# A scan over two directions: twelve loads per batch are issued by GpSimd and not by the sync engine

## The chip, the cores and the metric

The kernel runs on one core of one Trainium2 chip. The metric is the device time of one execution in microseconds (us), and lower is better. The engines are TensorE (PE, matrix products; PEld is its weight load), VectorE (DVE), ScalarE (ACT), GpSimd (POOL) and the sync engine (SP), which here only issues transfers. All of them run their own instruction stream in order and wait for each other through semaphores. A transfer (DMA) is issued by an engine's stream and then moves its bytes beside it.

## The reference, cut to what matters

The program is a first block (an RWKV mixer with a short convolution, then a convolutional feed-forward part) and a second one (attention). The part around the change is the RWKV scan, which runs once forwards and once backwards over 256 context and 1024 sequence tokens, with 8 heads of 64:

```
def wkv_scan(state0, r, decay, kk, b, v, k, reverse):
    def step(S, inp):
        r_t, w_t, kk_t, b_t, v_t, k_t = inp
        sa = jnp.einsum("bhvk,bhk->bhv", S, kk_t)
        S = (S * w_t[:, :, None, :] - sa[..., None] * b_t[:, :, None, :]
             + v_t[..., None] * k_t[:, :, None, :])
        return S, jnp.einsum("bhvk,bhk->bhv", S, r_t)
    xs = tuple(jnp.swapaxes(t, 0, 1) for t in (r, decay, kk, b, v, k))
    S, ys = lax.scan(step, state0, xs, reverse=reverse)
    return S, jnp.swapaxes(ys, 0, 1)
```

Everything before it (projections of the normed input) and after it (output projection, feed-forward part, attention) is untouched.

## The kernel before, in words

The program is one function after another: `projections` (names with `b_`), `scan` (`c_`), `mix_up` (`e_`), then the rest. Between two of them all engines meet at a barrier.

`scan` does the recurrence in chunks of C = 64 tokens: STEPS = 20 steps, 4 of context and 16 of sequence, each for both directions x = 0 and 1. Within a chunk the recurrence needs the inverse of a 64x64 triangular matrix for every head and direction. The 20 steps are taken in NBATCH = 5 batches T of BATCH = 4 steps, and for each batch the 32x32 blocks of all its triangles are inverted together by VectorE, long before TensorE uses them:

- TensorE makes the triangles (`blocks`, L1235), ScalarE copies them to `c_raw`, SP stores them to `pb` (L1104) and loads them back one block per partition as `c_nb` (L1150).
- VectorE inverts in four parts (`blocks(T, part)`), one part behind the work of each of four steps. It writes `c_ui` and `c_ti`, the inverse and its transpose. The last part of batch T stands behind step 4T - 4.
- SP stores them to `ub` (L1154) and `tb` (L1156). In SP's `step(s)` this is done when (s + 3) % 4 is 0, so for s = 1, 5, 9, 13 and T = 1, 2, 3, 4.
- Twelve loads then scatter the blocks into the places where TensorE reads them: `load_inverse(T)`, that is 2 of `of_level` (L1098, into `c_td`) and 4 of `of_diag` (L1093, into `c_ud`) from `ub`, and the same from `tb`. Each of the twelve moves 64 KB as 32 partitions x 16 blocks x 32 numbers, so 512 runs of 128 bytes. Before the first six SP waits for the landing of `ub`, before the last six for that of `tb`. They increment a semaphore `inv{T % 2}_{x}`.
- TensorE's step s makes the products of step s and then those of the next step u = s + 1. `level_y(x, u)` (L1264, `c_ps<-c_td,c_lm`) is the first that reads `c_td` and `c_ud` of batch u // 4. It waits for all six loads of its direction x, so for u = 4, 8, 12 and 16, in steps 3, 7, 11 and 15, it needs what `load_inverse` of T = 1 to 4 brought.

The twelve loads of T = 0 are another matter: they are issued ahead of the steps, half by SP and half by ScalarE.

SP also loads the operands of step s + 2 in step s (`load`, L1120 `c_op` of 512 KB and L1121 `c_vz` of 128 KB, for each direction), and `load_inverse` stands in its stream ahead of the loads of the next step. `load` waits until TensorE has used the slot (`p_s`, `p_y`). After step 10 SP loads `c_hc`, after steps 11 and 17 `c_w_raw`, which GpSimd splits into a high and a low part (L1591 to L1598). SP's last loads of `c_w_raw` wait for these splits. Beside them and five clears at the start, GpSimd has nothing to do in `scan`.

Descriptors for transfers that GpSimd issues are kept in memory that the kernel reserves where it makes the program (the line is in both versions):

```
nc = bacc.Bacc("TRN2", target_bir_lowering=False, num_devices=1, dynamic_dma_scratch_size=1024)
```

Of the kernel before, what the change touches and what calls it, by code (L numbers as in the profile page):

```python
# [1032 lines left out]
def scan(nc, d, t):  # L1033

    DIRS, HEADS = range(2), range(2)
    ROWS = [slice(HEAD * h, HEAD * h + HEAD) for h in HEADS]
    BATCH = 4
    NBATCH = STEPS // BATCH
# [4 lines left out]
    with ExitStack() as st:  # L1043
        sem = Sems(nc, st, "c_")
# [28 lines left out]
        S = lambda name, x: sem(f"{name}{x}")  # L1073
# [16 lines left out]
        def of_diag(eng, T, x, src):  # L1090
            for h in HEADS:
                for b in range(2):
                    eng.dma_start(ud[x][T % 2][quarter(h, b), :, :, cols32(b)].rearrange("p j q c -> p (j q) c"),  # L1093
                                  d[src][T, x, h, b].rearrange("n r c -> r n c")).then_inc(S(f"inv{T % 2}_", x), 16)

        def of_level(eng, T, x, src):
            for h in HEADS:
                eng.dma_start(td[x][T % 2][level(x), :, :, cols32(h)].rearrange("p j q c -> p (j q) c"),  # L1098
                              d[src][T, x, h, x].rearrange("n r c -> r n c")).then_inc(S(f"inv{T % 2}_", x), 16)

        def store_raw_of(eng, T, x):
            for h in HEADS:
# [6 lines left out]
        @block.sync  # L1109
        def _(sp):  # L1110
            def wait(name, x, value):
                if value > 0:
                    sp.wait_ge(S(name, x), value)

            def load(x, u):

                slot = slot_of(x, u)
                wait("p_s", x, u - 2)
                wait("p_y", x, u - 2 - NCTX)
                sp.dma_start(op_ring[x][u % 3][:], d["ops"][x, :, slot]).then_inc(S(f"loaded{u % 3}_", x), 16)  # L1120
                sp.dma_start(vz[x][u % 3][OF_K[x]], d["vts"][slot].rearrange("(h p) q v -> p h (q v)", h=2)).then_inc(S(f"loaded{u % 3}_", x), 16)  # L1121

            def load_w1(n):
                if n >= 2:
                    sp.wait_ge(sem("w1_lo"), n - 1)
                done = sem(f"w1_raw{n}") if n < 3 else t["ahead"](f"w1_{n}")
                sp.dma_start(w1_raw[:, n % 2], d["w_out"][n // 2][:, n % 2, 0:KD // 2]).then_inc(done, 16)

            def load_conv():
                for k in range(KD // 2):  # L1130
                    sp.dma_start(hc[:, k, 1].bitcast(F32), d["mixd"][:, k]).then_inc(sem(f"hc{k}"), 16)

            def load_pre(i):
                for x in DIRS:
                    wait("p_pre", x, i - 3)
                    slot = min(slot_of(x, 2 * i), slot_of(x, 2 * i + 1))
                    sp.dma_start(pre_ring[x][i % 2][:].rearrange("p j q z -> p (j q) z"),
                                 d["ops"][x, :, slot:slot + 2, :, C:3 * C].rearrange("p j q z -> p (j q) z")).then_inc(S(f"pre{i % 2}_", x), 16)

            def store_raw(T):  # L1140

                for x in DIRS:
                    wait("raw", x, 2 * T)
                    store_raw_of(sp, T, x)

            def load_blocks(T):
                if T:
                    sp.wait_ge(sem("pb"), 128 * T)
                    sp.wait_ge(sem("w_last"), T)
                sp.dma_start(nb[:, 0:HB * HB], d["pb"][T].rearrange("x h b n r c -> (x h b n) (r c)")).then_inc(sem("nb"), 16)  # L1150

            def store_blocks(T):
                sp.wait_ge(sem("ui"), T + 1)
                sp.dma_start(d["ub"][T].rearrange("x h b n r c -> (x h b n) (r c)"), ui[:, 0:HB * HB]).then_inc(sem("ub"), 16)  # L1154
                sp.wait_ge(sem("ti"), T + 1)
                sp.dma_start(d["tb"][T].rearrange("x h b n r c -> (x h b n) (r c)"), ti[:, 0:HB * HB]).then_inc(sem("tb"), 16)  # L1156

            def load_inverse(T):

                for x in DIRS:  # L1160
                    wait("p_z", x, BATCH * (T - 1))
                sp.wait_ge(sem("ub"), 16 * (T + 1))
                of_level(sp, T, 1, "ub")
                of_diag(sp, T, 0, "ub")
                sp.wait_ge(sem("tb"), 16 * (T + 1))
                of_level(sp, T, 0, "tb")
                of_diag(sp, T, 1, "tb")

            def step(s):
                for x in DIRS:  # L1170
                    if s + 2 < STEPS:
                        load(x, s + 2)
                if s == 0:
                    store_raw(2)
                if s == 1:
                    load_blocks(2)
                if s - 1 in pres and pres[s - 1] % 2:
                    load_blocks(pres[s - 1] // 2)
                if (s + 3) % BATCH == 0 and s + 3 < STEPS:
                    store_blocks((s + 3) // BATCH)  # L1180
                    load_inverse((s + 3) // BATCH)
                if s == 10:
                    load_conv()
                if s == 11:
                    for x in DIRS:
                        wait("p_pre", x, 2 * NBATCH - 2)
                    for n in range(2):
                        load_w1(n)
                if s == 17:
                    for n in range(2, 5):  # L1190
                        load_w1(n)
                if s in pres:
                    if pres[s] % 2:
                        store_raw(pres[s] // 2)
                    if pres[s] + 2 < 2 * NBATCH:
                        load_pre(pres[s] + 2)

            load_blocks(0)
            for x in DIRS:
                load(x, 0)  # L1200
            load_pre(2)
            load_pre(3)
            for x in DIRS:
                load(x, 1)
            for h in HEADS:
                sp.dma_start(t["pend"][ROWS[h], 1, NCTX:SLOTS], d["pends"][ROWS[1 - h]]).then_inc(sem("pend"), 16)
            load_pre(4)
            load_pre(5)
            sp.wait_ge(sem("clear"), 4)
            store_blocks(0)  # L1210
            load_blocks(1)
            sp.wait_ge(sem("ub"), 16)
            of_level(sp, 0, 1, "ub")
            of_diag(sp, 0, 0, "ub")
            load_pre(6)
            load_pre(7)
            for s in range(STEPS):
                step(s)

        @block.tensor  # L1220
        def _(pe):
            def wait(name, x, value):
                if value > 0:
                    pe.wait_ge(S(name, x), value)
# [32 lines left out]
            def level_y(x, u):  # L1257

                wait("lm", x, 2 * u + 2)
                wait(f"inv{u // BATCH % 2}_", x, 96 * (u // BATCH // 2 + 1))  # L1260
                j = place(x, u)
                for q in range(PAIRS):
                    for h in HEADS:
                        mm = nc.tensor.matmul(first(bank[x][0])[quarter(h, 1 - x), q],  # L1264
                                              lm[x][u % 2][level(x), h, q, W_KK[x], cols32(1 - x)],
                                              td[x][u // BATCH % 2][level(x), j, q, cols32(h)], start=True, stop=True)
                mm.then_inc(S("p_yd", x), 1)
# [78 lines left out]
            for s in range(STEPS):  # L1346
                u, more = s + 1, s + 1 < STEPS
# [235 lines left out]
        @block.gpsimd  # L1583
        def _(pool):
            for x in DIRS:
                for par in range(2):
                    nc.gpsimd.memset(ud[x][par][:], 0.0).then_inc(sem("clear"), 1)
                nc.gpsimd.memset(sc[x][0][:], 0.0).then_inc(S("sc", x), 1)
            for k in range(KD // 2):
                pool.wait_ge(sem(f"hc{k}"), 16)  # L1590
                nc.gpsimd.tensor_copy(hc[:, k, 0], hc[:, k, 1].bitcast(F32)).then_inc(sem("hc_hi"), 1)  # L1591
                pool.wait_ge(sem("hc_hi"), k + 1)
                nc.gpsimd.tensor_tensor(hc[:, k, 1], hc[:, k, 1].bitcast(F32), hc[:, k, 0].bitcast(F32), ALU.subtract).then_inc(sem("hc_lo"), 1)
            for n in range(3):
                pool.wait_ge(sem(f"w1_raw{n}"), 16)
                nc.gpsimd.tensor_copy(w1_hi[:, n], w1_raw[:, n % 2]).then_inc(sem("w1_hi"), 1)
                pool.wait_ge(sem("w1_hi"), n + 1)
                nc.gpsimd.tensor_tensor(w1_lo[:, n], w1_raw[:, n % 2], w1_hi[:, n].bitcast(F32), ALU.subtract).then_inc(sem("w1_lo"), 1)  # L1598
# [2102 lines left out]
```

## Time and profile before

| what | value |
|---|---|
| median of 3 runs | 2266.69 us (2255.43, 2266.69, 2269.16) |
| the profiled execution, span from first to last instruction | 2265.7 us |
| mean granted TensorE clock in it | 0.957 of full |
| PE, DVE, ACT, POOL busy in it | 2050.2, 1500.4, 892.1, 773.6 us |
| transfers in it | 271.16 MB, mean 120 GB/s |
| `scan` in it (TensorE's first product of its steps to the barrier) | some 498 to 750 us |

The profile has no device time of its own for the profiled execution beside its span of 2265.7 us; the span is 1.0 us under the median of the runs. In the rows below a time is counted from the start of the span, the second number of a timeline row is its length, and an arrow in brackets names what ended the idle time before a piece.

### The profile page before, as it was taken

The numbers are of one execution on the slowest core, as the hardware profiler recorded it, in microseconds if no ns is written. First come the engines' busy times: TensorE is split into PE (matmuls) and PEld (weight loads), VectorE is DVE, ScalarE is ACT, GpSimd is POOL, SyncE is SP. The second block draws the span as 40 slices with busy tenths as digits, with TensorE's granted clock in tenths as the row PEclk, the third lists the DMA queues.
The fourth block names the chain that finished last, engine by engine and source line by source line (L and its number), as shares of the span: only waits on it lengthen the run. The fifth ranks groups of instructions, "written<-read, shape, count | busy, mean of one in ns | idle before, by whom it ended". The sixth has DMA issues, their size and how long they took to land. (4 is left out here: it accounts for less than half of the span.)

```text
span 2265.7 us, 37012 instructions
## 1 busy us (share of the span) xinstructions
PE 2050.2 (90%) x15072; PEld 1594.0 (70%) x15072; DVE 1500.4 (66%) x2052; ACT 892.1 (39%) x1445; POOL 773.6 (34%) x460
## 2 busy tenths in 40 slices
PE   4989999837878898999999979999899999999898
PEld 1767677636767676788877768887677776776566
DVE  5777767679774548788988870454746676546644
ACT  5453443414434637333333331443434354333320
POOL 1144433300030145877777724533321111111111
PEclk7999999958899999999999999999999999999899
DMA  7535444597655422122221274523211111102512
GB/s 308 182 122 174 151 141 130 154 264 197 167 177 143 159 75 75 56 84 84 84 76 73 84 272 139 177 73 122 85 56 56 66 38 47 66 19 84 195 47 84
DMA packets 181335, 271.16 MB, mean 120 GB/s; under 512 B 74280, under 2 KB 122024, under 8 KB 176816
## 3 DMA queue, kind: packets, MB, share of 16 engines
q1 hardware_dynamic: 164816, 250.57, 33.9%
q10 hardware_dynamic: 16352, 18.22, 2.7%
q8 instruction: 121, 1.98, 0.4%
q14 instruction: 46, 0.38, 0.1%
HBM read 200.53 MB, written 68.23 MB: 119 GB/s over the span
## 5 line engine op out<-in xcount | busy, mean ns | idle before, releaser
L105 PE MATMUL b_ps<-h_hi,b_wpool 128*128 128x512 f32 (+1 forms) x896 | 277.4, 387 | 10.8 <-POOL b_wpool L744 10.8
L2995 PE MATMUL g_ps<-g_h_hi,w 128*128 128x512 f32 x784 | 260.0, 403 | 6.0 <-ACT g_q L3192 5.9
L3313 POOL TENSOR_TENSOR w<-raw_down,w 128x1024 fp32r<-128x1024 f32 x38 | 94.5, 2488 | 464.6 <-ACT w L3168 464.6
L2262 DVE SCALAR_TENSOR_TENSOR e_vars<-grid,vec,e_vars 128x1024 f32<-128x1024 f32 x168 | 216.0, 1285 | 7.4 <-ACT e_vars L2009 4.2
L105 PEld LDWEIGHTS b_ps<-h_hi,b_wpool 128*128 128x128 f32 x896 | 167.8, 192 | 56.3 <-POOL b_wpool L744 14.4
L2995 PEld LDWEIGHTS g_ps<-g_h_hi,w 128*128 128x128 f32 x784 | 149.3, 190 | 40.8 <-ACT g_q L3192 6.9
L105 PE MATMUL b_ps<-h_lo,b_wpool 128*128 128x512 f32 (+1 forms) x448 | 170.6, 381 | 0.0
L2995 PE MATMUL g_ps<-g_h_lo,w 128*128 128x512 f32 x392 | 156.1, 398 | 0.0
L2674 POOL TENSOR_TENSOR g_down_lo<-raw_down,g_down_hi 128x1408 fp32r<-128x1408 f32 x26 | 86.7, 3339 | 142.5 <-ACT g_down_hi L2574 142.5
L2513 PE MATMUL g_pb<-g_z_hi,g_down_hi 128*128 128x512 f32 x286 | 114.8, 401 | 14.7 <-DVE g_down_lo L2751 9.8
L744 POOL TENSOR_TENSOR b_wpool<-raw_in,b_wpool 128x1024 fp32r<-128x1024 f32 x26 | 67.9, 2611 | 173.2 <-ACT b_wpool L530 173.2
L2513 PE MATMUL g_pb<-g_z_hi,g_down_lo 128*128 128x512 f32 x286 | 113.1, 396 | 0.0
L2513 PE MATMUL g_pb<-g_z_lo,g_down_hi 128*128 128x512 f32 x286 | 112.7, 394 | 0.0
L1989 ACT ACTIVATE e_main_hi<-e_raw_up 128x512 fp32r<-128x512 f32 x68 | 41.9, 622 | 171.2 <-DMA e_raw_up<-w_ffn 168.9
L2103 POOL TENSOR_TENSOR e_main_lo<-e_raw_up,e_main_hi 128x512 fp32r<-128x512 f32 x68 | 92.6, 1365 | 16.0 <-ACT e_main_hi L1989 16.0
L105 PEld LDWEIGHTS b_ps<-h_lo,b_wpool 128*128 128x128 f32 x448 | 86.0, 192 | 15.7 <-issue 1.0
L3090 PE MATMUL g_ps<-g_h_hi,w 128*128 128x512 f32 x224 | 78.5, 421 | 9.1 <-DVE g_sq L3473 3.3
L2995 PEld LDWEIGHTS g_ps<-g_h_lo,w 128*128 128x128 f32 x392 | 74.5, 190 | 16.2 <-issue 0.5
L3465 DVE COPY g_pt<-g_pb 128x512 f32<-128x512 f32 (+2 forms) x144 | 74.2, 552 | 16.6 <-PE g_pb L3056 15.5
L1473 DVE TENSOR_TENSOR c_lm<-c_ps,con_mixer 128x512 f32<-128x512 f32 x80 | 50.7, 684 | 48.6 <-PE c_ps L1253 48.3
L2311 DVE TENSOR_TENSOR e_z<-e_act_g,combine 128x512 f32<-128x512 f32 x42 | 63.9, 1561 | 21.3 <-ACT e_act_g L2022 21.3
L3222 ACT ACTIVATE g_s<-g_logits,g_mx 128x128 f32<-128x128 f32 (+7 forms) x64 | 49.7, 777 | 69.0 <-DVE g_mx L3446 67.5
(524 smaller groups left out, 5284.4 us busy)
## 6 DMA issues: line engine op xcount, KB each, us to landing
e_raw_up<-w_ffn SPq DMA_DIRECT2D x22, 1024.0 KB, 4.9
raw_down<-w_down SPq DMA_DIRECT2D x32, 704.0 KB, 4.2
c_op<-ops SPq DMA_DIRECT2D x40, 512.0 KB, 5.0
raw_down<-w SPq DMA_DIRECT2D x38, 512.0 KB, 3.7
raw_in<-w SPq DMA_DIRECT2D x26, 512.0 KB, 4.2
mod_stage<-ada_rows ACTq DMA_DIRECT2D x24, 512.0 KB, 3.7
zs<-e_z SPq DMA_DIRECT2D x21, 512.0 KB, 2.6
ops<-b_xin SPq DMA_DIRECT2D x20, 512.0 KB, 4.7
```

Source lines behind the costliest of these rows:

```text
L105: last = nc.tensor.matmul(out, w[:, k, :], x[:, k, cols], start=(k == 0 and n == 0), stop=(k == nk - 1 and n == 2))
L744: TT(weights(s)[1], raw, weights(s)[0].bitcast(F32), ALU.subtract).then_inc(sem("lo"), 1)
L1473: TT(lm[x][u % 2][:, h], quad(bank[x][h]), bc(t["c_tri"][:, x], 1, PAIRS), ALU.mult).then_inc(S("lm", x), 1)
L2103: TT(w_lo[slot], a_of[slot] if i < PLAIN else source[slot], w_hi[slot].bitcast(F32), ALU.subtract).then_inc(sem(f"w_lo{slot}"), 1)
L2262: STT(out=acc, in0=view, scalar=wt, in1=acc, op0=ALU.mult, op1=ALU.add).then_inc(sem("conv"), 1)
L2311: a = TT(z[:, cols(g)], act_g[:, cols(g)], val_of(g, i), ALU.mult)
L2513: mm = nc.tensor.matmul(bank_of(g, j), w[s][:, k], y[:, f], start=(f == 0 and i == 0), stop=(f == NFF - 1 and i == 2))
L2674: nc.gpsimd.tensor_tensor(w_lo[w_slot(n)], raw[:, n % 2], w_hi[w_slot(n)].bitcast(F32), ALU.subtract).then_inc(sem(f"w_lo{n % 2}"), 1)
L2995: mm = nc.tensor.matmul(out_bank, ww[w % 2][:, k], xx[g][:, k], start=(k == 0 and a == 0), stop=(k == KD - 1 and a == 2))
L3090: mm = nc.tensor.matmul(ps[1][:], ww[w % 2][:, k], xx[g][:, k], start=(a == 0 and b == 0), stop=(a == 1 + LAST and b == 2))
L3313: nc.gpsimd.tensor_tensor(w_lo[w % 2], raw[:, w % 2], w_hi[w % 2].bitcast(F32), ALU.subtract).then_inc(sem("lo"), 1)
L3465: nc.vector.tensor_copy(pt[:, h, at // P:to // P].rearrange("p b c -> p (b c)"), turned[u % 2][:, 0:to - at]).then_inc(sem("unturned"), 1)
```

## The change

`load_inverse` is taken out of SP's stream. GpSimd's stream now has the loads of T = 1, 2, 3 and 4 one batch after another, behind its clears and ahead of the splits of `c_hc` and `c_w_raw`. The waits inside it are the same. Each batch has semaphores of its own (`inv{T}_{x}`, counted to 96) where two were used in turn. SP's `step` keeps the two stores.

```
@@ of_diag, of_level
-                                  d[src][T, x, h, b].rearrange("n r c -> r n c")).then_inc(S(f"inv{T % 2}_", x), 16)
+                                  d[src][T, x, h, b].rearrange("n r c -> r n c")).then_inc(S(f"inv{T}_", x), 16)
...
@@ block.sync
-            def load_inverse(T):
-
-                for x in DIRS:
-                    wait("p_z", x, BATCH * (T - 1))
-                sp.wait_ge(sem("ub"), 16 * (T + 1))
-                of_level(sp, T, 1, "ub")
-                of_diag(sp, T, 0, "ub")
-                sp.wait_ge(sem("tb"), 16 * (T + 1))
-                of_level(sp, T, 0, "tb")
-                of_diag(sp, T, 1, "tb")
...
                 if (s + 3) % BATCH == 0 and s + 3 < STEPS:
                     store_blocks((s + 3) // BATCH)
-                    load_inverse((s + 3) // BATCH)
...
@@ block.tensor, level_y
-                wait(f"inv{u // BATCH % 2}_", x, 96 * (u // BATCH // 2 + 1))
+                wait(f"inv{u // BATCH}_", x, 96)
...
@@ block.gpsimd
                 nc.gpsimd.memset(sc[x][0][:], 0.0).then_inc(S("sc", x), 1)
+            def load_inverse(T):
+
+                for x in DIRS:
+                    if T > 1:
+                        pool.wait_ge(S("p_z", x), BATCH * (T - 1))
+                pool.wait_ge(sem("ub"), 16 * (T + 1))
+                of_level(nc.gpsimd, T, 1, "ub")
+                of_diag(nc.gpsimd, T, 0, "ub")
+                pool.wait_ge(sem("tb"), 16 * (T + 1))
+                of_level(nc.gpsimd, T, 0, "tb")
+                of_diag(nc.gpsimd, T, 1, "tb")
+
+            for T in range(1, NBATCH):
+                load_inverse(T)
             for k in range(KD // 2):
                 pool.wait_ge(sem(f"hc{k}"), 16)
```

On SP, around step 1, the stream before (the stores of T = 1, the twelve loads, then the operands of step 4):

```order
L1154 DMA ub<-c_ui 128x1024
L1156 DMA tb<-c_ti 128x1024
L1098 DMA c_td<-ub 32x16x32 x2
L1093 DMA c_ud<-ub 32x16x32 x4
L1098 DMA c_td<-tb 32x16x32 x2
L1093 DMA c_ud<-tb 32x16x32 x4
L1120 DMA c_op<-ops 128x1024
L1121 DMA c_vz<-vts 64x2x256
L1120 DMA c_op<-ops 128x1024
L1121 DMA c_vz<-vts 64x2x256
```

The same place on SP in the changed kernel:

```order
L1154 DMA ub<-c_ui 128x1024
L1156 DMA tb<-c_ti 128x1024
L1120 DMA c_op<-ops 128x1024
L1121 DMA c_vz<-vts 64x2x256
L1120 DMA c_op<-ops 128x1024
L1121 DMA c_vz<-vts 64x2x256
```

The operand loads of the next step now follow the stores at once; this is so at all four places.

On GpSimd, from its last clear on, before:

```order
L1588 MEMSET c_sc 128x256
L1591 CAST c_hc<-c_hc 128x1024
L1593 TENSOR_TENSOR c_hc<-c_hc 128x1024
L1591 CAST c_hc<-c_hc 128x1024
L1593 TENSOR_TENSOR c_hc<-c_hc 128x1024
```

And in the changed kernel, from the loads of T = 4 on (the same four rows stand three times ahead of them, for T = 1, 2 and 3):

```order
L1098 DMA c_td<-ub 32x16x32 x2
L1093 DMA c_ud<-ub 32x16x32 x4
L1098 DMA c_td<-tb 32x16x32 x2
L1093 DMA c_ud<-tb 32x16x32 x4
L1593 CAST c_hc<-c_hc 128x1024
L1595 TENSOR_TENSOR c_hc<-c_hc 128x1024
L1593 CAST c_hc<-c_hc 128x1024
L1595 TENSOR_TENSOR c_hc<-c_hc 128x1024
```

All 48 loads stand ahead of GpSimd's first split, which could start when `c_hc` had landed and now comes after batch 4.

## Rows read from the trace of the kernel before

**Rows 1.** The page: busy time and share of each engine, and the transfer queues.

```profile
PE 2050.2 (90%) x15072; PEld 1594.0 (70%) x15072; DVE 1500.4 (66%) x2052; ACT 892.1 (39%) x1445; POOL 773.6 (34%) x460
...
q1 hardware_dynamic: 164816, 250.57, 33.9%
q10 hardware_dynamic: 16352, 18.22, 2.7%
```

**Rows 2.** Windows: stretch, its us, busy us by engine, granted clock, DMA share, GB/s.

```profile
490.00:750.00 260.00, 203.41 (x5924) 178.24 (x5916) 185.52 (x343) 103.47 (x304) 22.03 (x14) 0.89 0.62 172
...
497.00:549.00 52.00, 38.80 (x1022) 34.03 (x1026) 49.44 (x97) 20.19 (x59) 0.00 (x0) 0.77 0.82 222
```

**Rows 3.** Waits in 490 to 745 us: total, times, longest.

```profile
PE c_ps L1264 <- DVE c_lm L1473: 11.3, 6, 6.7
PE c_ps L1264 <- DMA c_ud<-ub: 7.3, 1, 7.3
PE c_ps L1246 <- DMA c_vz<-vts: 2.4, 2, 1.4
PE c_ps L1264 <- DMA c_ud<-tb: 1.4, 1, 1.4
```

**Rows 4.** Timeline of SP: each batch's first loads, and batch 1's last group.

```profile
527.00 0.92 SPq L1098 DMA_DIRECT2D c_td<-ub  x2
...
531.14 3.29 SPq L1093 DMA_DIRECT2D c_ud<-tb  x4
...
573.80 0.85 SPq L1098 DMA_DIRECT2D c_td<-ub  x2
...
626.84 1.14 SPq L1098 DMA_DIRECT2D c_td<-ub  x2
...
682.46 2.04 SPq L1098 DMA_DIRECT2D c_td<-ub  x2
```

**Rows 5.** Timeline of TensorE: the first product that needs each batch.

```profile
549.62 0.28 PE L1264 MATMUL c_ps<-c_td,c_lm 32*32 32x32 f32 x5
...
604.60 0.61 PE L1264 MATMUL c_ps<-c_td,c_lm 32*32 32x32 f32 x32
...
655.04 0.81 PE L1264 MATMUL c_ps<-c_td,c_lm 32*32 32x32 f32 x32
...
704.55 0.82 PE L1264 MATMUL c_ps<-c_td,c_lm 32*32 32x32 f32 x32
```

**Rows 6.** DMA issues: issuing queue, count, KB each, median us from issue to landing.

```profile
c_ud<-ub SPq DMA_DIRECT2D x20, 64.0 KB, 2.4
...
c_ud<-tb ACTq DMA_DIRECT2D x4, 64.0 KB, 3.6
```

**Rows 7.** Line L1093: duration of an issue, and its time to landing (smallest, median, largest).

```profile
L1093 SPq DMA_DIRECT2D c_ud<-ub x20: 484/488/1236, 492.4 to 686.1; - x20
...
DMA to landing us min/median/max: 2.2/2.4/4.7
```

**Rows 8.** Timeline of TensorE after an idle time, and the same products later.

```profile
526.03 0.64 PE L1264 MATMUL c_ps<-c_td,c_lm 32*32 32x32 f32 x16 [6.73 <-DVE c_lm L1473]
...
529.87 1.97 PE L1246 MATMUL c_ps<-con,c_op 128*128 128x128 f32 x8
...
552.40 1.09 PE L1246 MATMUL c_ps<-con,c_op 128*128 128x128 f32 x8
```

**Rows 9.** Windows, columns as in Rows 2: the stretch after that idle time, and the next.

```profile
526.00:534.50 8.50, 7.91 (x152) 6.97 (x152) 7.99 (x31) 3.48 (x10) 0.00 (x0) 0.52 0.71 162
534.50:549.00 14.50, 12.28 (x408) 10.76 (x410) 13.57 (x24) 6.94 (x20) 0.00 (x0) 1.00 0.95 266
```

**Rows 10.** Timeline of GpSimd: its first split, its sixth and its last.

```profile
644.07 1.94 POOL L1591 CAST c_hc<-c_hc 128x1024 fp32r<-128x1024 f32 x1 [180.16 <-DMA c_hc<-mixd]
...
663.42 1.27 POOL L1598 TENSOR_TENSOR c_w_lo<-c_w_raw,c_w_hi 128x512 fp32r<-128x512 f32 x1
...
727.99 0.61 POOL L1596 CAST c_w_hi<-c_w_raw 128x512 fp32r<-128x512 f32 x1 [63.29 <-DMA c_w_raw<-w_out]
```

More of the change, by code:

```diff
@@ L1098, in of_level @@
                 eng.dma_start(td[x][T % 2][level(x), :, :, cols32(h)].rearrange("p j q c -> p (j q) c"),
-                              d[src][T, x, h, x].rearrange("n r c -> r n c")).then_inc(S(f"inv{T % 2}_", x), 16)
+                              d[src][T, x, h, x].rearrange("n r c -> r n c")).then_inc(S(f"inv{T}_", x), 16)
         def store_raw_of(eng, T, x):
```

## The prediction

> **What bounds the kernel now.** Read the engines first: TensorE is busy for 90% of the span, and all transfers come from two hardware queues, SP's and ACT's; GpSimd's has none [rows 1]. So nothing in this profile shows what a transfer issued by GpSimd costs, and that is the number on which everything below hangs. Then the stretch of the scan: in 260 us TensorE is busy for 203.41 and VectorE for 185.52, GpSimd for 22.03 [rows 2]. Neither engine is full, since each step is a chain that goes back and forth between TensorE, ScalarE and VectorE. A delay put into TensorE's stream there moves the end of the scan, and the barrier behind it hands this on to the rest of the kernel one for one.
>
> The waits say which delays come from transfers: TensorE waited 7.3 and 1.4 us for the scattered inverse, each once, both for batch 0, which the change leaves alone; and 2.4 us in two waits for the operands c_vz [rows 3]. For batches 1 to 4 it never waited. The reader is to see how much room there was: SP issued the first load of a batch at 527.00, 573.80, 626.84 and 682.46 us [rows 4], and the first product that needs the batch ran at 549.62, 604.60, 655.04 and 704.55 us [rows 5]. The differences are 22.6, 30.8, 28.2 and 22.1 us, 103.7 in all. These starts are not SP's to choose: they are when the store of ub had landed, so GpSimd cannot begin earlier, and its clears at the start of the scan are long over.
>
> **What is removed.** SP loses 12 issues in each of four batches. In batch 1 they fill 527.00 to 534.43 us [rows 4], 7.4 us. What stands behind them is the operand load of the next step. The most that can come of it is the two waits of TensorE for c_vz, 2.4 us [rows 3]. Where SP was late for no one, nothing is gained. The two stores of a batch stay on SP. The semaphores of their own cost nothing: the waits of TensorE are as many as before.
>
> **What is added.** GpSimd issues 48 loads, and waits for ub, tb and, for T above 1, for TensorE's p_z of the batch before the last, which is long done when ub lands. Let p be the time from one load to the next on GpSimd. TensorE's second direction needs the last of the twelve, so it stalls in a batch by 12p less the room of that batch. Below 22.1/12 = 1.84 us no batch stalls; above 30.8/12 = 2.57 us all four do, and the stall is 48p - 103.7 us. The sum is steep: a tenth of a microsecond in p is 4.8 us in the kernel.
>
> The bounds for p from rows: from below the issue on SP, 0.49 us [rows 7], if GpSimd only has to issue and the loads overlap as they do on SP. From above the longest landing of such a load, 4.7 us [rows 7], if each has to land before the next is made. I take the second picture, since the memory for descriptors that this kernel reserves is small, 1024 bytes, and each load is 512 runs. With one load at a time p is about a landing plus what comes ahead of it. The same load landed 2.4 us after its issue from SP and 3.6 us from ACT [rows 6]; I take the middle, 3.0 us. It is a choice: 2.4 is from a queue whose issue is cheap, and the 3.6 is from four loads at the start of the scan.
>
> The Trainium skill has the reason in "DMA: Bandwidth & Descriptors", sections "SWDGE vs HWDGE vs iDMA" and "Terms": a transfer issued by GpSimd has its descriptors written by software into a ring in SBUF, one queue of it, a descriptor being 16 bytes. By it 1024 bytes are an estimated 64 places for each of the 16 transfer engines and direction, and a load of 512 runs takes 32 of them and one for its completion, 33, so that two loads (66) do not fit. No row here shows this, as no row has such a queue.
>
> With p = 3.0 the twelve take 36 us, and the stalls are 13.4, 5.2, 7.8 and 13.9 us, 40.3 in all (48 x 3.0 - 103.7). One correction to it: the start of batch 2 at 573.80 us came late behind its store in a crowded moment, and with the stall of batch 1 ahead of it the crowd is another one. I take 2 us off.
>
> **What a stall costs beside itself.** After 6.73 us of idleness TensorE's eight transposes took 1.97 us against 1.09 later [rows 8]. The granted clock was 0.52 in the 8.5 us after it, which is the level of 1.2 GHz, and 1.00, 2.4 GHz, after that [rows 9]. TensorE was busy for 7.91 of these 8.5 us; at the full level this work takes 4.1, and as a part of it is hidden behind VectorE and ScalarE I count 3 us for a stall, 12 for four.
>
> **What the moved splits cost.** GpSimd's splits ran from 644.07 to 664.7 us and needed then 20.6 us [rows 10]. Now they wait for batch 4. With p = 3.0 that ends at 682.46 + 36 = 718.5 us on the old clock, the splits at 739, the last one, which needs one more load, at some 746; TensorE's scan ends 14 us later than before on the same clock, at 763. So they are hidden, with 17 us to spare, and a larger p moves both ends alike. The cover would be gone if the splits took twice their time beside VectorE. They no longer run beside VectorE at steps 11 and 12 but later: nothing either way.
>
> **The sum.** 40.3 - 2 + 12 = 50 us. The 2.4 us that SP could give back are not subtracted: both waits stand just ahead of a stall, which takes up what they free. The profiled span becomes 2265.7 + 50 = 2316 us. As this span is 1.0 us under the median of the runs, the forecast on the median is 2317 us, 2.2% slower.
>
> **The rivals.**
>
> *The loads overlap, and nothing happens.* If GpSimd makes the next load while the one before flies, p is its issue alone. Below 1.84 us there is no stall, and the time is 2266.7 - 2.4 = 2264 us at best, 2267 if the waits for c_vz turn into others. For it speaks that SP does just this (twelve in 7.4 us, each landing in 2.4), against it only the small descriptor memory. The Trainium skill speaks for this side, and for no effect: "DMA: Bandwidth & Descriptors", section "Issuing engines are not separate DMA queues", says that issuing from several engines saves only the sequencer's time, which is usually small. This is the case that ends on the other side of the forecast; the point from which it decides is p = 1.84 us.
>
> *One at a time, but quick.* At p = 2.4 (SP's median landing) the stalls are 6.2, 0, 0.6 and 6.7 us, and with the clock of two real stalls (6 us) the time is 2267 + 13.5 + 6 = 2286 us, just under 1%.
>
> *One at a time, and slow.* VectorE was busy for 49.44 of the 52 us in which batch 1 falls, and the transfer engines for 0.82 of them [rows 2]. If VectorE or the crowd holds up GpSimd, p = 4.0 gives 48 x 4.0 - 103.7 + 12 = 100 us, 2367 us; the bound 4.7 gives 134 us, 2401 us. In the Trainium skill, "SBUF — State Buffer", the box on the "DVE blocks DMA" trap says that VectorE's two-port instructions keep GpSimd from writing descriptors. VectorE's instructions here are mostly of another kind, and no row shows GpSimd held up by them.
>
> *A gain above 1%.* It would need 23 us, ten times what TensorE waited for any transfer that the change touches.
>
> **How the numbers follow.** One at a time with p from 2.6 to 3.6 us: 0.50 (48p - 103.7 + 10, so 31 to 79 us on 2267). Overlapping loads, no stall: 0.27. One at a time with p under 2.6: 0.11, half of it below 1%. Slow, p above 3.6: 0.11. A gain over 1%: 0.01. The range is from 2258 us (the no-stall case with the spread that the three runs show) to 2350 us, p = 3.6; it leaves out the slow case. A measurement of this kernel can tell about 1% from no change. Slower by over 1% is 0.50 + 0.11 + 0.06 = 0.67, within 1% 0.32, faster 0.01. The likeliest case alone has 2298 to 2346 us.
>
> **What would show it.** In the profile of the changed kernel GpSimd's loads should stand some 3 us apart, with 36 us from the first to the last landing of a batch, against 7.4 us of issue on SP. TensorE should wait at L1264 for a transfer into c_ud of tb in steps 3, 7, 11 and 15, longest in the first and the last, and its clock should drop behind each. The waits for c_vz should be gone, and SP should wait for GpSimd's split in step 17 for longer than before. The forecast is wrong if the loads stand less than 1.84 us apart, and its size is wrong by 48 times the error in p.

## The result and the profile after

The changed kernel takes 2328.62 us, the median of 4 runs (2326.62 to 2330.29), against 2267.93 us for the kernel before (4 runs, 2255.43 to 2273.80). The ratio is 1.0267, with a 95% interval of 1.0243 to 1.0292: 60.7 us slower. The profiled execution has a span of 2324.8 us, 59.1 more than the 2265.7 of before. The lines that TensorE, ScalarE and VectorE have in the scan stand 12 lower in the changed file: L1264, the product with c_td, is now L1252, L1246 is L1234, L1473 is L1461. GpSimd's splits stand two higher (L1591 is L1593).

The page of the changed kernel, busy time of the engines and the queues (they answer to [rows 1]). A queue written by software is new, with the 3.15 MB of the 48 loads; the work of TensorE, VectorE and ScalarE is what it was. GpSimd is busy for 27.3 us more: the 48 issues take 31.6 us, and its other work took 4.3 us less.

```profile
PE 2052.3 (88%) x15072; PEld 1598.8 (69%) x15072; DVE 1497.9 (64%) x2052; ACT 892.2 (38%) x1445; POOL 800.9 (34%) x508
...
q1 hardware_dynamic: 139472, 247.43, 32.1%
q10 hardware_dynamic: 16352, 18.22, 2.6%
q0 software_dynamic: 1536, 3.15, 0.5%
```

GpSimd's timeline in the changed kernel: parts of batch 1, the last loads of batch 4, and the first split behind them. Columns: start, duration, then in brackets the idle time before it and what ended that.

```profile
524.69 0.83 POOL L1098 DMA_DIRECT2D c_td<-ub  x1 [65.00 <-DMA ub<-c_ui]
531.34 0.66 POOL L1098 DMA_DIRECT2D c_td<-ub  x1 [5.82 <-issue]
533.94 0.65 POOL L1093 DMA_DIRECT2D c_ud<-ub  x1 [1.94 <-issue]
...
569.45 0.66 POOL L1093 DMA_DIRECT2D c_ud<-tb  x1 [1.84 <-issue]
...
759.07 0.65 POOL L1093 DMA_DIRECT2D c_ud<-tb  x1 [1.97 <-issue]
759.72 1.05 POOL L1593 CAST c_hc<-c_hc 128x1024 fp32r<-128x1024 f32 x1
```

The reader is to see "x1" in every row and the idle time between the rows. An issue keeps GpSimd for 0.65 us, and then it sits for 1.8 to 6.3 us before the next, though it waits for no semaphore there; that is why the view can say no more than "issue". From its first issue to its last a batch now takes 44.8, 36.5, 41.0 and 35.6 us, where SP issued batch 1 in 7.4. The split, which is no transfer, follows the last load without a gap: what holds GpSimd up stands in the way of its next transfer and not of its next computation.

TensorE's timeline, the products at which each direction needs the new batch, for batches 1 to 4 (answers to [rows 5]), and the first transposes behind the first stall:

```profile
556.08 0.63 PE L1252 MATMUL c_ps<-c_td,c_lm 32*32 32x32 f32 x16 [7.40 <-DMA c_td<-tb]
...
571.79 0.50 PE L1252 MATMUL c_ps<-c_td,c_lm 32*32 32x32 f32 x11 [15.08 <-DMA c_ud<-tb]
...
574.43 1.86 PE L1234 MATMUL c_ps<-con,c_op 128*128 128x128 f32 x8
...
622.71 0.44 PE L1252 MATMUL c_ps<-c_td,c_lm 32*32 32x32 f32 x16 [0.81 <-DMA c_td<-tb]
633.78 0.64 PE L1252 MATMUL c_ps<-c_td,c_lm 32*32 32x32 f32 x16 [10.63 <-DMA c_ud<-tb]
...
689.19 0.64 PE L1252 MATMUL c_ps<-c_td,c_lm 32*32 32x32 f32 x16 [3.87 <-DMA c_td<-tb]
699.52 0.64 PE L1252 MATMUL c_ps<-c_td,c_lm 32*32 32x32 f32 x16 [9.70 <-DMA c_ud<-tb]
...
751.22 0.64 PE L1252 MATMUL c_ps<-c_td,c_lm 32*32 32x32 f32 x16 [6.87 <-DMA c_td<-tb]
...
761.45 0.64 PE L1252 MATMUL c_ps<-c_td,c_lm 32*32 32x32 f32 x16 [9.59 <-DMA c_ud<-tb]
```

Each batch stops TensorE twice, first for the direction whose tb part is c_td, then for the other. Together these are 22.5, 11.4, 13.6 and 16.5 us, 64.0 in all, against none before. The waits of the scan (494.9 to 809 us; total, times, longest):

```profile
DVE c_lm L1461 <- PE c_ps L1241: 92.3, 30, 23.0
...
PE c_ps L1252 <- DMA c_ud<-tb: 47.4, 5, 15.1
...
PE c_ps L1252 <- DMA c_td<-tb: 19.0, 4, 7.4
...
PE c_ps L1252 <- DVE c_lm L1461: 5.5, 2, 4.9
```

One of the five waits for c_ud of tb, 2.4 us, is batch 0's. TensorE's waits for c_vz are gone, and its wait for VectorE's c_lm is 5.5 us where it was 11.3 [rows 3]. VectorE's own longest wait is now 23.0 us, where TensorE stands still for batch 1.

Now the scan cut at the stalls. First the kernel before, with the five stretches that end where each batch's first product ran (columns as in [rows 2]), its first stretch and the sum:

```profile
498.45:549.62 51.17, 39.42 (x1056) 34.56 (x1056) 48.68 (x92) 19.80 (x58) 0.00 (x0) 0.78 0.80 219
...
sum 252.53, PE 202.29 PEld 177.28 DVE 181.23 ACT 102.39 POOL 22.03; mean PE 40.46 PEld 35.46 DVE 36.25 ACT 20.48 POOL 4.41
```

The changed kernel, the same stretches without the stalls:

```profile
495.20:548.68 53.48, 42.00 (x1056) 36.94 (x1056) 50.49 (x96) 19.86 (x58) 4.11 (x6) 0.76 0.71 204
571.79:621.90 50.11, 43.72 (x1232) 38.99 (x1232) 33.31 (x70) 21.60 (x63) 5.23 (x8) 0.86 0.37 113
...
sum 247.34, PE 208.57 PEld 184.85 DVE 156.34 ACT 99.21 POOL 35.48; mean PE 41.71 PEld 36.97 DVE 31.27 ACT 19.84 POOL 7.10
```

And the four stalls alone:

```profile
548.68:571.79 23.11, 0.63 (x16) 0.56 (x17) 6.25 (x4) 1.36 (x3) 3.92 (x6) 0.57 0.66 168
...
sum 66.29, PE 2.36 PEld 2.07 DVE 23.78 ACT 3.28 POOL 15.37; mean PE 0.59 PEld 0.52 DVE 5.95 ACT 0.82 POOL 3.84
```

The sum closes: 66.3 us of stalls (the 64.0 us of waits and the few products between them), and 5.2 us less between them (252.5 to 247.3), so 61.1 us for the scan. The span grew by 59.1; the rest is that this execution reached the scan 3.25 us earlier and took 1.2 us longer behind it, small beside the spread of the runs of the kernel before (2255.43 to 2273.80).

### The profile page after: what moved, and what is told of

Read it like the earlier page. It is cut to its first block and busy times, and to the rows that moved or that the text cites. A ratio compares the mean times of both kernels' runs of the same rounds, so it can differ in the third digit from the quotient of the medians.

```text
span 2324.8 us, 37012 instructions
## 1 busy us (share of the span) xinstructions
PE 2052.3 (88%) x15072; PEld 1598.8 (69%) x15072; DVE 1497.9 (64%) x2052; ACT 892.2 (38%) x1445; POOL 800.9 (34%) x508
## 3 DMA queue, kind: packets, MB, share of 16 engines
q0 software_dynamic: 1536, 3.15, 0.5%
## 5 line engine op out<-in xcount | busy, mean ns | idle before, releaser
L105 PEld LDWEIGHTS b_ps<-h_hi,b_wpool 128*128 128x128 f32 x896 | 166.4, 190 | 55.7 <-POOL b_wpool L744 14.6
L2997 PEld LDWEIGHTS g_ps<-g_h_hi,w 128*128 128x128 f32 x784 | 149.1, 190 | 40.3 <-ACT g_q L3194 6.6
L2515 PE MATMUL g_pb<-g_z_hi,g_down_hi 128*128 128x512 f32 x286 | 115.1, 402 | 14.8 <-DVE g_down_lo L2753 9.8
L1461 DVE TENSOR_TENSOR c_lm<-c_ps,con_mixer 128x512 f32<-128x512 f32 x80 | 51.1, 685 | 92.4 <-PE c_ps L1241 92.3
L1252 PE MATMUL c_ps<-c_td,c_lm 32*32 32x32 f32 x640 | 18.1, 208 | 83.1 <-DMA c_ud<-tb 47.4
```

Of the source, the lines that this page charges most:

```text
L105: last = nc.tensor.matmul(out, w[:, k, :], x[:, k, cols], start=(k == 0 and n == 0), stop=(k == nk - 1 and n == 2))
L1461: TT(lm[x][u % 2][:, h], quad(bank[x][h]), bc(t["c_tri"][:, x], 1, PAIRS), ALU.mult).then_inc(S("lm", x), 1)
L2515: mm = nc.tensor.matmul(bank_of(g, j), w[s][:, k], y[:, f], start=(f == 0 and i == 0), stop=(f == NFF - 1 and i == 2))
L2997: mm = nc.tensor.matmul(out_bank, ww[w % 2][:, k], xx[g][:, k], start=(k == 0 and a == 0), stop=(k == KD - 1 and a == 2))
```

## The experiments

The kernel before is timed beside each of them, with medians of 2265.5 to 2266.4 us. Where no interval is given there was one run. Single runs of the kernel before lay up to 12.5 us from its median. So beside the times stands, where it helps, what the trace says of the scan alone, from TensorE's first product of its steps to its last: 250.7 us in the kernel before (250.1 to 254.2 in the four other runs that keep the loads, have no late batch and no extra traffic), 311.7 in the changed kernel.

**Memory for two more loads.** The changed kernel with one line different:

```
-    nc = bacc.Bacc("TRN2", target_bir_lowering=False, num_devices=1, dynamic_dma_scratch_size=1024)
+    nc = bacc.Bacc("TRN2", target_bir_lowering=False, num_devices=1, dynamic_dma_scratch_size=2048)
```

> The changed kernel with 2048 bytes of descriptor memory in place of 1024. Theory A (the memory holds one load of 512 runs and not two, so that each load waits for the landing of the one before): GpSimd's loads then stand about 1 us apart (0.65 us of issue and a little), a batch is issued in some 12 us instead of 36 to 45, TensorE waits for none of them, and the time is that of the kernel before within 0.3%, 2261 to 2270 us. Theory B (GpSimd makes descriptors slowly, or the crowd on the transfer engines holds them up, whatever the memory): the spacing stays 3.3 to 4.1 us and the time near 2327 us. Theory C (it is the place in GpSimd's stream or the semaphores): also near 2327 us.

Measured: 2270.70 us (10 runs), ratio to the kernel before 1.002 (1.0007 to 1.0034). That is 57.9 us less than the changed kernel and 4.5 more than the kernel before beside it, just above the range that I had given. GpSimd's timeline for batch 1:

```profile
528.45 1.48 POOL L1098 DMA_DIRECT2D c_td<-ub  x2 [66.09 <-DMA ub<-c_ui]
529.92 0.65 POOL L1093 DMA_DIRECT2D c_ud<-ub  x1
536.75 1.30 POOL L1093 DMA_DIRECT2D c_ud<-ub  x2 [6.18 <-issue]
...
549.53 1.93 POOL L1093 DMA_DIRECT2D c_ud<-tb  x3 [6.28 <-issue]
```

Loads now leave in groups of up to three, with the idle time between the groups. A batch takes 23 to 25 us from first issue to last, not the 12 that I had expected of three in flight, so TensorE still waits for two of the four batches, 6.6 us, and the scan takes 257.3 us, 6.6 more than before. What settles the time is the memory, not that GpSimd issues.

**64 bytes more.** The same line with 1088 instead of 1024, which is 68 places for each of the 16 transfer engines if a place is 16 bytes.

> The changed kernel with 1088 bytes, 64 more. If a place is 16 bytes and a load takes 33 places (512 runs over 16 transfer engines, and one for its completion), two loads need 66 places: 1024 bytes have 64, 1088 have 68. Theory A with this count: two loads fit, the spacing falls from a landing (2.5 us and more) to half a landing or to the issue, 1.0 to 1.8 us, and most of the stall of 64 us goes: 2265 to 2285 us. Theory A with another count (a place kept free, or more places for a load): as at 1024, 2327 us. Theory B: 2327 us.

Measured: 2290.50 us, 38 us less than the changed kernel, for 64 bytes. Every row of all four batches is a pair:

```profile
529.91 1.48 POOL L1098 DMA_DIRECT2D c_td<-ub  x2 [65.17 <-DMA ub<-c_ui]
537.39 1.30 POOL L1093 DMA_DIRECT2D c_ud<-ub  x2 [6.00 <-issue]
540.81 1.30 POOL L1093 DMA_DIRECT2D c_ud<-ub  x2 [2.12 <-issue]
```

So the threshold lies above 64 places and at 68 or under, where 66 had been worked out. The time is 5 us above the range that I had given. The loads stood 2.2 to 2.7 us apart on the mean, not the 1.0 to 1.8 of the expectation, and yet TensorE waited only 11.2 us for batches 1 to 4, and the scan took 265.3 us, 14.6 more than before. The span is 23.0 us longer than before; the other 8.4 us lie ahead of the scan and behind it, where the two kernels do the same. In a single run they say nothing of the loads.

**The wait made by hand.** With 2048 bytes, so that memory no longer decides, GpSimd waits for the landing of each load before it issues the next:

```
+            def one(T, x, dst, src):
+                nc.gpsimd.dma_start(dst, src).then_inc(S(f"inv{T}_", x), 16)
+                landed[T, x] = landed.get((T, x), 0) + 16
+                pool.wait_ge(S(f"inv{T}_", x), landed[T, x])
```

> 2048 bytes as in e1, but GpSimd's stream waits for the landing of each load before it issues the next. Theory A: this is by hand what the small memory does, so spacing 2.5 to 4.1 us and the stalls of TensorE are back, 55 to 75 us in all, 2320 to 2335 us. If e1 is fast for another reason than overlap (another address of a buffer, say), this one stays fast as well.

Measured: 2328.06 us, the changed kernel's time to 0.6 us. The 44 idle times between the loads are 130.5 us in all, against 129.0 in the changed kernel, and as there is a semaphore now, the view can name them:

```profile
534.39 0.66 POOL L1580 DMA_DIRECT2D c_td<-ub  x1 [6.05 <-DMA c_td<-ub]
536.97 0.65 POOL L1580 DMA_DIRECT2D c_ud<-ub  x1 [1.92 <-DMA c_td<-ub]
```

What the changed kernel's "issue" hid is therefore worth a wait for the landing of the load before. One thing differs: TensorE's waits for batches 1 to 4 are 76.4 us here and 64.0 there, at the same time of the kernel. The part on the prediction comes back to this.

**The semaphores alone.** The kernel before, with `inv{T}_` for `inv{T % 2}_` and the matching wait in level_y; the loads stay on SP.

> The kernel before with the semaphores of the change alone: inv{T} of its own for each batch, the loads still on SP. All theories but C: the kernel before within 0.3%, since every wait is met at the same moment. Theory C in the form that the semaphores matter: a difference of more than 0.5% either way.

Measured: 2266.64 us (10 runs), ratio 0.9995 (0.9974 to 1.0016). The semaphores cost nothing that can be told.

**Halves.** At 1024 bytes each load is cut in two, 24 loads of 32 KB for a batch:

```
-                of_diag(nc.gpsimd, T, 0, "ub")
+                diag_halves(T, 0, "ub")
...
+            def diag_halves(T, x, src):
+                for h in HEADS:
+                    for b in range(2):
+                        for i in range(2):
+                            nc.gpsimd.dma_start(ud[x][T % 2][quarter(h, b), 2 * i:2 * i + 2, :, cols32(b)].rearrange("p j q c -> p (j q) c"),
+                                                d[src][T, x, h, b, 8 * i:8 * i + 8].rearrange("n r c -> r n c")).then_inc(S(f"inv{T}_", x), 16)
```

> The changed kernel with its 1024 bytes, each of GpSimd's loads cut in two of 256 runs (24 loads of 32 KB for a batch, the same bytes). By the count that e1 and e2 bear out (runs / 16 + 1 places of 64) a half takes 17 places, so three are in flight where one whole load was, and a batch is eight groups of three: 8 x (3 x 0.65 + some 2.5 us) = 36 us at most, 28 us if the landings of a group are quicker, against 36 to 45 now. The stalls of TensorE fall from 64 us to 10 to 40 us, the time to 2275 to 2310 us. A theory in which GpSimd's time goes by loads and not by places expects 24 x 3.5 = 84 us for a batch and 2500 us.

Measured: 2321.92 us, only 7 us less than the changed kernel, where 2275 to 2310 was expected. This expectation missed.

```profile
526.59 1.93 POOL L1587 DMA_DIRECT2D c_td<-ub  x3 [63.47 <-DMA ub<-c_ui]
...
551.22 1.74 POOL L1587 DMA_DIRECT2D c_td<-tb  x3 [1.95 <-issue]
555.38 1.74 POOL L1581 DMA_DIRECT2D c_ud<-tb  x3 [2.41 <-issue]
561.11 1.73 POOL L1581 DMA_DIRECT2D c_ud<-tb  x3 [3.99 <-issue]
```

The count is right again: a half takes 17 places by the same rule, 51 for three, 68 for four, and there are three at a time. But a wait between two groups is much as before (1.9 to 4.0 us in these rows, up to 6.4), although each half carries 32 KB and not 64. Over the four batches the mean wait is 2.96 us (32 of them) and in the changed kernel 2.93 (44). So what is paid is a landing for each filling of the memory, hardly its bytes. There are fewer fillings, 34 us less of waiting in all, but the 96 issues take 24 us more than the 48 did: batch 1 takes 43.1 us from first issue to last, as against 44.8.

**Half of the loads on each engine.** At 1024 bytes the six loads from ub stay on GpSimd, the six from tb go back to SP, with a semaphore of their own.

```
+                    wait(f"inv{u // BATCH}_", x, (64, 32)[x])
+                    wait(f"sp_inv{u // BATCH}_", x, (32, 64)[x])
```

> Each queue takes one half: the six loads from ub stay on GpSimd (1024 bytes, one at a time), the six from tb are back on SP. Theory: TensorE stalls only by what a batch's loads on GpSimd exceed the room of 21 to 29 us. Six loads at 3.3 to 4.1 us are 20 to 25 us, so batches 1 to 3 have room and batch 4 stalls by 0 to 4 us: 2266 to 2274 us. If the cost were in each load on GpSimd and not in the lateness of the last one, half of the 60 us would stay: 2297 us.

Measured: 2268.87 us (10 runs), ratio 0.9996 (0.998 to 1.0012). TensorE waits for no batch from 1 to 4. GpSimd's six loads still go one by one (526.55 to 549.1 us in batch 1), but six of them end about when the room ends. The slow loads cost nothing that can be told as long as the last is in time: it is lateness that is paid.

**4096 bytes.**

> The changed kernel with 4096 bytes, 256 places: seven loads in flight. GpSimd issues a batch in 8 us and one landing, and no batch is late. e1 (three in flight) still had GpSimd's last loads land 27 to 31 us after the first and TensorE waiting 6.6 us for tb in batches 1 and 4; if that is its 0.2%, this kernel has the time of the kernel before less at most 2.4 us, ratio 0.997 to 1.001. If the 0.2% comes from elsewhere (GpSimd's splits moved to late steps, its loads beside SP's), it stays at 1.002.

Measured: 2268.04 us (12 runs), ratio 1.0006 (0.999 to 1.0021). A batch takes 12 to 14 us from first issue to last:

```profile
523.32 1.49 POOL L1098 DMA_DIRECT2D c_td<-ub  x2 [63.65 <-DMA ub<-c_ui]
524.80 2.57 POOL L1093 DMA_DIRECT2D c_ud<-ub  x4
527.36 0.65 POOL L1098 DMA_DIRECT2D c_td<-tb  x1
531.31 0.66 POOL L1098 DMA_DIRECT2D c_td<-tb  x1 [3.30 <-issue]
```

Seven loads leave without a gap (2, 4 and 1), and the eighth waits, as it does for 0.35 us in batch 2: 256 places hold seven times 33 and not eight. In batches 3 and 4 nine leave without a gap, and the tenth waits; nine issues take 5.8 us, so that the first loads can have landed by then (the shortest landing is 2.2 us). No stall is left, and no gain either. TensorE's waits for c_vz are there again, 2.7 us in two, although the operand loads stand ahead as in the changed kernel: it is not the order on SP alone that takes them away.

**No loads at all.** The changed kernel without the 48 loads of batches 1 to 4; the second places of c_td are cleared instead, so those steps work with values that are not the inverse's.

> Left out: all twelve loads of batches 1 to 4, on any engine, so that TensorE multiplies with the parts of batch 0, with zeros and with old parts. It bounds from above what any place for these loads can give. Theory: SP's 30 us of issue in the scan hid behind TensorE but for the 2.4 us that it waited for c_vz, so ratio 0.996 to 1.000 against the kernel before. If SP's stream or the small transfers held up more than the waits show, below 0.99.

Measured: 2264.53 us (12 runs), ratio 0.9984 (0.9968 to 1.0001). Whoever issues these loads, and however well, there are some 1.8 us to be had from them, at the interval's end 7 us.

**A denser crowd.** SP loads 1 MB more in each of steps 0 to 9, into a part of c_hc that is free then, read by no one; once in the changed kernel, once in the kernel before.

```
+                if s < 10:
...
+                    for x in DIRS:
+                        sp.dma_start(hc[:, x, 1].bitcast(F32), d["ops"][x, :, slot_of(x, s + 2)].rearrange("p q z -> p (q z)")).then_inc(sem("extra"), 16)
```

> The changed kernel with 1 MB more on SP's queue in each of steps 0 to 9: two loads of 512 KB from ops into a part of c_hc that is free until step 10 (their data are not used). SP's own loads of a step are 1.25 MB. In the changed kernel GpSimd's loads stood 2.5 us apart when SP was quiet and 5 to 7 us when SP had just issued; batches 1 to 4 took 47, 39, 43 and 38 us with transfer engines busy for 0.62, 0.40, 0.46 and 0.32. Theory: the price above 30 us is the crowd, each landing queueing behind SP's bytes, so batches 1 to 3 grow by 4 to 15 us each and batch 4 (steps 13 to 15, no extra loads) stays at 38 us; time 2340 to 2370 us. Rival (VectorE or GpSimd's own descriptor writing sets the price above 30 us): batches 1 to 3 unchanged, and the time within 10 us of 2327 us.

> The control to e9: the same extra 1 MB for each step in the kernel before, whose twelve loads are on SP. It shows what the extra loads cost by themselves (operands that come later, SP's time). Theory: rooms of 22 to 31 us against batches of 7.4 us of issue on SP, and one step of prefetch for the operands, cover most of it: 2267 to 2285 us, so that e9 minus this one exceeds the 60 us of the change. Rival: the extra loads cost as much here as in e9, and the difference stays at 60 us.

Measured: 2345.49 us for the changed kernel and 2274.74 for the one before, so the change costs 70.8 us in the crowd and 60.7 without. Both are single runs, and the difference of 10 us is no larger than the spread of such runs. The scans alone are 326.5 and 260.0 us, 66.6 apart, against 61.0 without the crowd. GpSimd's first and last load of batch 1:

```profile
529.78 0.83 POOL L1098 DMA_DIRECT2D c_td<-ub  x1 [66.81 <-DMA ub<-c_ui]
...
580.93 0.66 POOL L1093 DMA_DIRECT2D c_ud<-tb  x1 [1.89 <-issue]
```

First to last issue is 51.2, 44.2, 39.4 and 34.3 us for batches 1 to 4, against 44.8, 36.5, 41.0 and 35.6. Batches 1 and 2, beside which the extra bytes fly, grew by 6.4 and 7.7 us; batches 3 and 4, behind them, did not grow. That batch 3 would grow as well was expected and missed, since SP issued the last extra loads at 657.09 us, 17 us before batch 3's first. A landing in traffic is longer, and with one load at a time that is paid twelve times.

**SP in another order.** The kernel before, with the twelve loads issued behind the next step's operand loads and not ahead of them.

```
+                if (s + 2) % BATCH == 0 and s + 2 < STEPS:
+                    load_inverse((s + 2) // BATCH)
...
-                    load_inverse((s + 3) // BATCH)
```

> The kernel before with another order on SP: the twelve loads of a batch are issued in the next step, right behind the operand loads, and no longer ahead of them. This takes the operands past the twelve without any work for GpSimd, which is the use that the change could have had. By e8 (no loads at all: 0.9984, interval 0.9968 to 1.0001) there are at most some 4 us in it, and the waits for c_vz were 2.4 us: ratio 0.998 to 1.001, no difference that can be told. If the loads are now late instead, TensorE waits at L1264 and the ratio is above 1.001.

Measured: 2265.48 us (12 runs), ratio 0.9992 (0.9977 to 1.0008). The waits for c_vz are gone, as in the changed kernel, and nothing measurable comes of it. No version is faster than the kernel before by more than the intervals allow for chance.

## Why the prediction was right, and which of its terms were off

**The mechanism was right.** The decision was between loads that overlap and loads one at a time, taken from the size of the descriptor memory. Five counts bear it out: at 64 places one load of 33, at 68 two (66), at 128 three (99, and four would be 132), at 256 seven (231, not 264), and at 64 three of 17 (51, not 68). The counts allow 33 or 34 places for a whole load and 17 to 21 for a half. The waiting by hand gives the same time to 0.6 us. The Trainium skill's rule in "DMA: Bandwidth & Descriptors" (sections "SWDGE vs HWDGE vs iDMA" and "Terms"), from which the 33 places were estimated, agrees with all five. The section "Issuing engines are not separate DMA queues" of that page of the Trainium skill, which spoke for no effect, agrees with the run at 4096 bytes (1.0006) and the one with half of the loads on each engine (0.9996): where no load is late, it is indifferent in this kernel who issues.

**The term p was too small.** The prediction put it at 3.0 us, the middle between two landings. From a batch's first issue to the product that needed its last load it was 47.1, 38.9, 43.4 and 38.0 us, 167.3 in all, or 3.49 us for a load. That is inside the 2.6 to 3.6 of the chosen case, near its end. The prediction's formula with 3.49 gives 48 x 3.49 - 103.7 = 63.8 us of stalls, and 64.0 us of waits were measured; with 3.0 it gave 40.3. As p is taken here from the ends of the stalls, this tests only the rooms. They were 24.0, 27.0, 29.2 and 20.9 us, 101.1 in all, near the 103.7 read ahead. So the term of the stalls failed in one number, and the 0.49 us in it are worth 23.5 us. The upper bound for one load, 4.7 us from [rows 7], did not hold either: idle times reached 6.34 us and one landing 6.7. It held for the mean of a batch.

What made p large is the traffic. Windows of the changed kernel from first issue to about the last landing, columns as in [rows 2], batches 1 to 4:

```profile
524.69:572.00 47.31, 22.16 (x600) 19.75 (x602) 28.55 (x59) 11.39 (x32) 8.03 (x12) 0.68 0.62 172
594.88:634.00 39.12, 24.31 (x705) 21.73 (x699) 27.09 (x54) 12.52 (x35) 7.84 (x12) 0.76 0.40 103
656.16:700.00 43.84, 23.17 (x592) 20.35 (x587) 27.40 (x56) 10.60 (x31) 7.85 (x12) 0.75 0.46 140
723.47:762.00 38.53, 19.41 (x592) 17.07 (x592) 10.08 (x21) 9.04 (x27) 10.02 (x14) 0.80 0.32 91
```

The spacing of the loads is 4.07, 3.32, 3.73 and 3.24 us here and goes in the order of the share of the transfer engines (0.62, 0.40, 0.46, 0.32). It does not follow VectorE, which is busy for 0.69 of batch 2's window and 0.26 of batch 4's with nearly the same spacing. The crowd experiment shows the traffic's part directly. The second load of batch 1 left 6.7 us after the first; the last ones, in the quiet of batch 4, came every 2.5 to 2.6. The prediction had the crowd in hand, as the rival with p = 4.0 or more, and gave the main case the middle of two medians. VectorE can be told apart where the transfer engines are quiet. From 686.66 to 699.52 us it was busy for 7.38 of 12.86 us, with a transfer share of 0.10, and the loads left every 2.63 us; from 748.87 to 761.45 us it did nothing at a share of 0.11, and they left every 2.55. So no run here shows GpSimd held up by VectorE for more than some 0.1 us a load. Instructions of another kind than this kernel's were not tried.

**The clock's term of 12 us is not borne out.** The clock did fall, as predicted: behind the four stalls the granted clock was 0.50, the level of 1.2 GHz, for the first 3.7 to 5.6 us in which TensorE worked again, and eight transposes behind the first stall took 1.86 us, like those behind the idle time in [rows 8]. What this cost can't be read off. TensorE's busy time in the scan rose from 202.3 to 210.9 us, but 2.6 of these 8.6 us lie ahead of the first stall (42.00 against 39.42 us for 1056 products each). The kernels that keep the loads and have no late batch range from 202.1 to 206.7 us. And the kernel that waits by hand, with the same falls of the clock and longer stalls, has 200.8.

**A stall's length is not its price.** The next batch's loads can't start before TensorE has gone on and the work up to the next store of ub is done. So the scan is made of the stretches from a batch's first issue to the product that needs its last load, and of those from this product to the next batch's first issue, or to the end. The first kind are 103.7 us before, 167.3 in the changed kernel and 169.1 when waiting by hand, and the second kind 118.5, 114.9 and 115.1. With what lies ahead of batch 1 (28.5, 29.5 and 29.0 us) that makes 250.7, 311.7 and 313.2. The stretches behind the stalls did not become longer, as the prediction's 12 us would have it, but 3.5 us shorter. By hand TensorE came to its stalls some 11 us earlier in all, waited 76.4 us and not 64.0, and gained nothing, as the loads ended no sooner. The windows show how the work moved: VectorE did 23.8 us of its work inside the stalls and only 156.3 between them, where it had 181.2, and TensorE's time without work between the stalls fell from 50.2 us (252.5 less 202.3) to 38.8 (247.3 less 208.6). That this is why the slower clock left no trace was not tried by itself and rests on the windows.

**The correction of -2 us for batch 2's start** went the wrong way: batch 2's room came out as 27.0 us and not 30.8, which lengthens its stall.

**So two errors cancelled in part.** The stalls, 66.3 us with the few products between them, are 26 us over the forecast, and clock and correction, 5 us less where 10 more were forecast, are 15 us under it: 50 forecast, 61 measured in the scan. The forecast of 2317 us was 11.6 us low, half a per cent; that it came so near is in part luck.

**The smaller steps.** The splits were hidden, as said: GpSimd's last one ended at 785.3 us and the scan at 808.8. The c_vz waits went, as said, and were worth nothing that can be told; the run without loads bounds them. That SP would wait longer for GpSimd's split was wrong: it waited 5.6 us where it had waited 7.2. That the longest stalls would be the first and the last batch's was right for the whole of a batch (22.5 and 16.5 us), since these have the least room. But the prediction counted only the wait for c_ud of tb, and that is shortest in the last batch (15.1, 10.6, 9.7 and 9.6 us): each batch first stops TensorE for c_td of tb, which the prediction did not name.

```profile
SPq L1127 <- POOL c_w_lo L1600: 5.6, 1, 5.6
```

```profile
783.94 1.33 POOL L1600 TENSOR_TENSOR c_w_lo<-c_w_raw,c_w_hi 128x512 fp32r<-128x512 f32 x1
```

## What to carry to other kernels

Before a load goes to GpSimd, count its runs against the descriptor memory that the kernel reserves: if a second load doesn't fit, each one waits for the landing of the one before, and the price is (number of loads) x (landing in that traffic) less the room up to the first use. Read the room as two times in the trace, when the source is there and when the first user runs; take the landing stretch by stretch, from rows beside the traffic of that stretch. Here the loads stood 2.5 to 2.6 us apart in the quiet and up to 7.0 beside SP's transfers, and neither the queue's median (2.4) nor its longest landing (4.7) would have given the 3.49. And where the next round's transfers wait for the work behind a stall, do not add up the stalls: follow the chain from transfer to transfer. Stalls of 64.0 and of 76.4 us cost this kernel the same to 1.5 us of the scan.

## What the runs showed of the hardware that was not expected

64 bytes of descriptor memory are worth 38 us in this kernel by the time of a single run (2328.6 to 2290.5), and 46 by the length of the scan (311.7 to 265.3). The next 960 are worth another 20 by the time and 8 by the scan (257.3).

The issue of such a load takes 0.65 us on GpSimd against 0.49 on SP [rows 7], and its landing has a longer tail. Line L1093 on GpSimd, ub's loads, in the changed kernel (the landing below is for ub's and tb's together; the median for ub's alone is 3.6 us, beside SP's traffic, and 2.3 for tb's):

```profile
L1093 POOL DMA_DIRECT2D c_ud<-ub x16: 648/652/660, 533.9 to 742.7; - x16
...
DMA to landing us min/median/max: 2.2/2.6/6.7
```

Loads of half the size with three in flight are waited for as long as one whole load: 2.96 us on the mean against 2.93, and the kernel takes 2321.9 us. And room for three loads does not cut a batch to a third: with three in flight at 2048 bytes twelve loads need 23 to 25 us, since a wait is longer than with one: 4.3 us on the mean of 16, up to 7.2, against 2.9 of 44, up to 6.3. Only seven in flight brought it to 12 to 14 us.
